# Three blocks on one Trainium2 core: the order of the experts' spill units and of their weight loads

## The reference, cut to what matters

```python
def _hier_moe(h, w_rg, b_rg, w_re, b_re, w1, w3, w2):
    g_top = argmax(hf @ w_rg + b_rg)                  # one of 4 groups
    e_in = (hf @ w_re + b_re)[g_top's 4 experts]
    top_v, top_j = lax.top_k(e_in, 2)                 # two experts of the group
    w_sel = softmax(top_v) * gate_g
    ...
    for e in range(16):
        he = silu(hf @ w1[e]) * (hf @ w3[e])          # 1024 -> 512
        y = y + combine[:, e:e + 1] * (he @ w2[e])    # 512 -> 1024
    return y
```

## Time and profile before

| | us |
|---|---|
| median of 3 runs | 1707.56 |
| lowest, highest | 1704.43, 1712.65 |
| profiled execution, its own time | 1712.39 |
| its span, first to last instruction | 1710.6 |
| TensorE busy in the span | 1627.8 (95%) |
| VectorE, ScalarE, POOL busy | 700.6, 257.3, 110.4 |
| mean granted clock of TensorE | 0.981 of full |

### The profile page before, as it was taken

One profiled execution on the slowest core, in us unless ns is written; L12 is line 12 of the kernel. 1 busy time (PEld: TensorE's weight loads), 2 busy tenths in 40 slices (PEclk: granted clock), 3 DMA queues, 4 the chain that ended last, 5 costly groups with the idle time before them and its releaser, 6 DMA issues.

```text
span 1710.6 us, 17491 instructions
## 1 busy us (share of the span) xinstructions
PE 1627.8 (95%) x6984; PEld 880.4 (51%) x6984; DVE 700.6 (41%) x1332; ACT 257.3 (15%) x580; POOL 110.4 (6%) x125
## 2 busy tenths in 40 slices
PE   4999999999999999999989999999889988899997
PEld 2445556474444444445756788547765653233332
DVE  1617853568887100113164667003475444111112
ACT  3121113010000000000144110000131412010110
POOL 1000001100000000001000100000322101010101
PEclk9999999999999999999989999999999989999999
DMA  9453441146565421106710599532643257999996
GB/s 342 171 196 101 146 163 60 43 144 231 198 245 185 160 84 63 49 1 215 261 60 1 178 331 363 193 141 95 214 142 105 101 216 299 412 410 410 410 411 249
DMA packets 130658, 333.46 MB, mean 195 GB/s; under 512 B 15897, under 2 KB 16193, under 8 KB 117521
## 3 DMA queue, kind: packets, MB, share of 16 engines
q1 hardware_dynamic: 111488, 298.90, 47.0%
q0 software_dynamic: 18176, 30.27, 5.4%
q10 hardware_dynamic: 912, 3.17, 0.5%
HBM read 354.50 MB, written 15.49 MB: 216 GB/s over the span
## 4 chain that ended last, share of the span: by engine, by line
PE 86%; DMA 5%; DVE 4%; issue 2%; POOL 1%; SPq 1%; ACT 1%; DVEq 0%; POOLq 0%; ACTq 0%
PE psum L642 82%; PE psum L646 3%; DMA big<-x_slots 2%; DMA wring<-in_w_mod 1%; DMA wring<-in_mlp_w 1%; SPq L1474 1%; DMA y_slots<-gate 1%; DMA wring<-in_ev_w_in 1%; POOL small L1567 1%; ACT wide L1713 0%; DMA wide<-y_slots,slot_i 0%; DVE wide L2122 0%; DVE big L2459 0%; DVE big L2618 0%; ACT big L1713 0%
## 5 line engine op out<-in xcount | busy, mean ns | idle before, releaser
L642 PE MATMUL psum<-wring,big 128*128 128x512 f32 (+2 forms) x1600 | 559.5, 578 | 8.1 <-issue 5.9
L642 PE MATMUL psum<-wide,wring 128*128 128x256 f32 (+3 forms) x1872 | 490.2, 436 | 0.2
L642 PEld LDWEIGHTS psum<-wring,big 128*128 128x128 f32 (+1 forms) x1600 | 241.4, 173 | 302.8 <-issue 296.8
L642 PEld LDWEIGHTS psum<-wide,wring 128*128 128x128 f32 (+1 forms) x1872 | 303.5, 183 | 174.0 <-issue 145.2
L642 PE MATMUL psum<-wring,wide 128*128 128x512 f32 (+3 forms) x576 | 212.8, 573 | 8.5 <-DMA wring<-in_w_mod 4.9
L1713 ACT ACTIVATE big<-psum 128x512 f32<-128x512 f32 (+2 forms) x155 | 83.1, 546 | 669.4 <-PE psum L642 614.3
L2122 DVE SCALAR_TENSOR_TENSOR wide<-wring,csilu,wide 128x512 f32<-128x512 f32 x252 | 175.5, 748 | 3.0
L642 PEld LDWEIGHTS psum<-wring,wide 128*128 128x128 f32 (+1 forms) x576 | 95.7, 184 | 106.5 <-issue 93.8
L2223 DVE TENSOR_TENSOR wide<-psum,gate 128x512 f32<-128x512 f32 x27 | 18.6, 691 | 321.7 <-PE psum L642 321.5
L1567 POOL TENSOR_TENSOR small<-small 128x1 f32<-128x1 f32 (+2 forms) x30 | 41.2, 1373 | 1037.0 <-DVE small L2240 884.4
L1713 ACT ACTIVATE wide<-psum 128x256 f32<-128x256 f32 (+2 forms) x114 | 46.1, 418 | 306.0 <-PE psum L646 152.9
(11 more groups left out here) (277 smaller groups left out, 912.7 us busy)
## 6 DMA issues: line engine op xcount, KB each, us to landing
wring<-in_mlp_w SPq DMA_DIRECT2D x32, 2048.0 KB, 8.8
wring<-in_w SPq DMA_DIRECT2D x64, 1024.0 KB, 18.6
wring<-in_w_mod SPq DMA_DIRECT2D x24, 2048.0 KB, 13.1
big<-in_w SPq DMA_DIRECT2D x23, 2048.0 KB, 23.1
wide<-in_w SPq DMA_DIRECT2D x28, 1024.0 KB
wring<-in_w_ada SPq DMA_DIRECT2D x12, 2048.0 KB, 8.9
wring<-in_w_in SPq DMA_DIRECT2D x8, 2048.0 KB, 9.6
wring<-in_ev_w_in SPq DMA_DIRECT2D x6, 2048.0 KB, 13.4
```

The lines of the kernel that those rows point to most:

```text
L642: return nc.tensor.matmul(o, a, b, start=first, stop=last)
```

## The change

The order of the units changes in `moe_order()`. Before it was 0, 1, S0, 2, 3, S1, 4, 5, S2, ... 12, 13, S6, 14, 15. After it is 0, 1, 2, 3, S0, 4, 5, S1, 6, 7, S2, 8, 9, S3, 10, 11, S4, 12, 13, S5, S6, 14, 15. `AT`, `GROUP_ORDER`, `BEGINS`, the stores and the group loads follow from it. SP's list of loads is written anew to match.

```diff
     for e in range(NEXP):
         order.append(e)
-        if e % 2 == 1 and e // 2 < SPILLS:
-            order.append(NEXP + e // 2)
+        if e % 2 == 1 and 0 < e // 2 < SPILLS:
+            order.append(NEXP + e // 2 - 1)
+        if e == NEXP - LATE - 1:
+            order.append(NEXP + SPILLS - 1)
     return order
...
             load_up(0)
             load_down(0)
             load_up(1)
             load_down(1)
+            load_spill_down(0)
+            load_up(2)
+            load_up(3)
+            load_down(2)
             load_spill_up(0)
-            load_spill_down(0)
+            load_down(3)
             for k in range(SPILLS):
-                load_up(2 * k + 2)
-                if 0 < k:
-                    load_spill_down(k)
-                load_up(2 * k + 3)
-                load_down(2 * k + 2)
+                for e in (2 * k + 4, 2 * k + 5):
+                    if e < NEXP:
+                        load_up(e)
+                        load_down(e)
                 if k + 1 < SPILLS:
                     load_spill_up(k + 1)
-                load_down(2 * k + 3)
+                    load_spill_down(k + 1)
```

## The result

The changed kernel takes 1737.91 us (median of 4 runs, 1735.31 to 1740.33) against 1708.22 us (4 runs, 1704.43 to 1712.65): ratio 1.0157, interval 1.0135 to 1.0179, that is 23 to 31 us slower. The forecast had 1717.8 and a range up to 1723. The direction was right; the size was off by a factor of more than two.

What follows compares the result with a forecast made beforehand. In the experts' stage DMA at about 410 GB/s and TensorE were both taken to be at their limit; 14.0 us of slip less 3.8 us of gather lateness gave +10.2 on the 1707.56 median: 1717.8 us, range 1711 to 1723.

Steps and rivals of the forecast that it cites:

- Bytes ahead: Experts' stage: a load lands when the bytes queued before it have gone by; five early waits, 1.2 to 6.1 us.
- The seventh unit: Expert 5's unit in the new order: starts at 1510.9 against 1496.7 us in the old, a slip of 14.2 us.
- SP's order: SP's load list: w1/w3 loads issued 3.5 to 4.7 us late; priced at nothing, up to 1.5 us per five pairs.
- The backlog: DMA queue in the experts' stage: bytes still queued hide SP's later issues, 3 to 7 us of cover.
- the rival of the dry queue: SP's waits ahead of w1/w3 loads empty the DMA queue: +5 to +7 us on the main case, 1724; chance 0.13.
- its sign: DMA windows with a share below 0.95 between 1540 and 1670 us would show the dry queue.
- the main case: Whole kernel: slip of 12.5 to 16 us in the experts' stage, +8.7 to +12 us; chance 0.56.
- the six empty spill units: Experts' stage: 10.8 us of TensorE each and no DMA, pauses in which the DMA queue catches up.
- slow restart: TensorE after a wait: slow start of 1.46 us; after expert 5's wait 0 to 1.5, 1.4 together with later waits.
- the later waits: Odd experts after expert 5 meet the queue: 0.4 us or nothing, then about another 1 us; 1.4 with slow start.
- tail: Kernel's end: last store lands in about 4 us, TensorE becomes the later chain, 3.8 us of gather lateness is won back.

Runs made afterwards that it cites:

- e5: Changed kernel, but the first spill unit's weight loads are skipped by their condition, its overflow left out; 1.0047 of the kernel before, stage 286.6 us.
- e1: Changed kernel's order of units, with SP's loads listed in the order in which buffers come free; 1.0056 of the kernel before, stage 286.1 us.
- e2: Changed kernel with only the last spill unit's empty w1/w3 load moved ahead of expert 15's w2 load; 1.0117 of the kernel before, stage 296.1 us.
- second profile of before: The kernel before, unchanged, profiled once more; 1716.35 us in one run, stage 275.8 us.
- e9: e1 with the even expert's w2 load again ahead of the odd expert's w1/w3 loads; 1.0112 of the kernel before, stage 294.7 us.
- e6: Kernel before with the first spill unit's w2 load first in SP's list, waiting for the table alone; 0.9982 of the kernel before, stage 273.7 us.
- e4: Kernel before with an empty spill unit brought forward behind the first spill unit, SP's list matched; 1.0015 of the kernel before, stage 275.2 us.
- e10: e6 with POOL issuing each group's load one turn of its loop earlier; 0.9992 of the kernel before, stage 274.7 us.
- e3: Changed kernel, but the first spill unit's weight loads bring 16 of 128 partitions; 1.0112 of the kernel before, stage 293.1 us.

## Why the prediction was wrong

The first half held. *Bytes ahead*: waits of 4.5, 1.2, 6.1, 2.2 and 4.8 us were forecast before units 2, 3, S0, 4 and 5; measured 3.64, under 1, 5.58, 3.26 and 3.81. The seventh unit was to start 14.2 us later from the stage's start than before; it was 87.8 - 72.8 = 15.0. e5 shows that the waits before expert 2, S0 and expert 4 go with the bytes. That each size came within 1.1 us is partly luck: in the kernel before, on whose landings the sum was built, the wait before expert 2 was 5.92 us in one profile and 3.82 in the other. And one of these byte terms was a choice of the list, not of the order: D4 ahead of U5 costs a wait and a restart that e1 doesn't have.

The step that failed is *SP's order*, "I price it at nothing, and at up to 1.5 us for each of five pairs". Two things were missed in it.
- The backlog that was to hide the later issues isn't there once the empty units begin. The size of the delay was right: U7 is issued at 1526.69, 4.1 us after `up` of expert 5 freed its buffer at about 1522.6, where 3.5 to 4.7 were expected. The cover was not: the windows of 10 us show 302 and 340 GB/s, and U6 lands 4.5 us sooner after its issue than in e1. The waits before experts 9 and 13 are 1.72 + 1.35 = 3.1 us. This was the rival of the dry queue, at a chance of 0.13. It occurred beside the main case, with its sign (a DMA share of 0.93 in 1560 to 1570) and at about half of its price of 5 to 7 us.
- The empty loads. I had listed the six empty spill units as pauses without DMA and asked only about bytes. Their commands still set semaphores, and with S5 and S6 side by side the one for S6 had to be issued in one unit's time from behind D15: 4.4 us (e2). None of my rivals had it.

The *slow restart* behind the wait of expert 5 (1.77) and the later waits were to replace each other at 1.4 together. They added up instead: 1.8 + 3.1 + 4.4 = 9.3 us.

Of TensorE's clock the Trainium skill (TensorE: Matmul & The Clock Gate, What's actually happening) says that the throttled state is the default and activity releases it. The restarts of the changed kernel agree, 5.24 to 5.62 us behind waits of 2.75 to 5.58, with a granted clock of 0.64 to 0.69; but a wait of 3.82 in the second profile of before was followed by 3.65 at a granted clock of 1.00.

The *tail* was wrong by 3.2 us. I let the final adds start when the gathered rows are there, and overlooked that VectorE takes its instructions in order: the scaling of the last unit stands ahead of them and ends at 1724.20. Before, it ended at 1698.98 and the first add began at 1699.59, so only 0.6 us could be won by an earlier gather, and not 3.8. The chain that ends last runs through this scaling and the four adds, not through TensorE's last product, which ends at 1726.25, 3.1 us before the final adds. The store doesn't land in 4 us either, but in 8.7, with idle engines. And the 9.86 us of before, which I took for a landing in a full queue, were not that: the engines moved 338 GB/s from 1680 to 1685 and 156 from 1685 to 1690. The stores that were issued from 1589 to 1658, at 407 to 412 GB/s, took 24.6 to 29.6 us.

Summed: 10.2 forecast, + 0.8 on the seventh unit, + 7.9 on the restart and the later waits, + 3.2 in the tail make 22.1 of the 24.5 us between the two profiles. 1.9 are older than the stage, and 0.5 are small waits. The medians differ by 29.7, as the first profile of before was of an execution 4.2 us above its median and that of after of one 1.0 below.

The experiments divide the stage's loss otherwise than the change's name does: 9 us are the new order of units (e1), 8.6 the w2 load of the even expert ahead of the odd one's w1/w3 (e9), and 4.4 the last spill unit's command (e2). The remaining 1.4 (e9 against e2) is within what two profiles of one kernel differ by. In e9's exchange the waits and the restart that came back give 4.05 + 1.77 + 1.00 + 1.09 = 7.9 of the 8.6 us.

## What to carry to other kernels

In an in-order issue queue, write the loads in the order in which their buffers come free, and check every wait that is put ahead of another load: what it holds back counts even while the bytes seem to hide it, for the backlog is only as deep as the loads already issued. A load that moves nothing still has a command and a semaphore; give it the same due time as a real one. Where DMA and the engine are balanced, look for an idle stretch to move bytes into: here it gained 3 us (0.2%, e6), and none of the other orders gained anything. And before a gain is booked at the end, ask what stands ahead of the released instruction in its own queue.

## What the runs showed of the hardware

- A store of 0.26 MB to HBM from POOL's queue took 8.7 us to land with the engines nearly idle (25 GB/s, after), 12.1 us when they still moved 334 GB/s at its issue (e4), and 24.6 to 29.6 us in a full queue (before, 407 to 412 GB/s).
- Issuing a load isn't always cheap: the four of U5 took SP 10.70 us (2.1 to 3.5 us each), and 1.76 us in the kernel before. The DMA engines were full in both, so that alone isn't the reason; no run isolates it.
- Sixteen partitions in place of 128 brought the rate down to 160 GB/s at a busy share of 1.10 (e3).
- The restart at the lower clock isn't a fixed function of the wait: 5.27 us behind a wait of 2.16 (e10, granted clock 0.69) and 3.65 behind 3.82 (before, second profile, 1.00); 5.24 behind 2.75 (after) and 3.65 behind 2.77 (e3).
- The Trainium skill (DMA: Bandwidth & Descriptors, Where 436 GB/s comes from) has the HBM side bind at about 358 GB/s; this core moved 415 GB/s over 65 us (after, 1435 to 1500), and 410 and 411 in slice after slice of the kernel before.
